# A decoder step with cached attention: each gate group's cache copy cut into eight pieces, and value sums placed in four column groups

## What is computed

```
def dilated_attention_step(q, k, v, cache, win, dil, rel_bias, h0):
    t = q.shape[1]
    lc = cache.shape[1]
    n_keys = win // dil + 1
    kv_all = jnp.concatenate([cache, jnp.stack([k, v], axis=2)], axis=1)
    idx = lc + jnp.arange(t)[:, None] - jnp.arange(n_keys)[None, :] * dil
    kvg = jnp.take(kv_all, jnp.maximum(idx, 0), axis=1)
    s = jnp.einsum('bthd,btjhd->bhtj', q, kvg[:, :, :, 0]) * SCALE + bias[:, None, :]
    p, lse = softmax_weights(s, None)
    o = jnp.einsum('bhtj,btjhd->bthd', p, kvg[:, :, :, 1])
    return o, jnp.moveaxis(lse, 1, 2), kv_all[:, t:]
...
pa = oa.reshape(b, s, A_OUT_W) @ w_oa
pb = ob @ w_ob
mix = (jax.nn.sigmoid(ga) * pa + jax.nn.sigmoid(gb) * pb) @ w_out
h = layer_norm(ALPHA * x + mix, ln1_g, ln1_b)
gate, up = jnp.split(h @ w_ffn_in, 2, axis=-1)
return layer_norm(ALPHA * h + (jax.nn.silu(gate) * up) @ w_ffn_out, ln2_g, ln2_b)
```

## Time and profile before

| | |
|---|---|
| median of 3 runs | 1805.73 us (1802.27 to 1807.96) |
| the profiled execution | 1798.35 us, its span 1796.6 us |
| TensorE busy | 1746.7 us, 97% of the span |
| VectorE busy | 993.2 us, 55% |
| ScalarE busy | 702.5 us, 39% |
| mean busy share of the 16 DMA engines | 44.2% for SyncE's queue (q1), 15.4% for ScalarE's (q10), 10.9% for GpSimd's (q0) |

### The profile page before, as it was taken

The page is one execution under the profiler, slowest core; times in us unless marked ns, Lnnn a source line. Parts: engine busy times, 40 slices in busy tenths (PEclk is TensorE's granted clock), DMA queues, the critical chain, the costliest instruction groups (busy, mean ns, idle before and its releaser), DMA issues.

```text
span 1796.6 us, 32525 instructions
## 1 busy us (share of the span) xinstructions
PE 1746.7 (97%) x12511; PEld 1661.9 (93%) x12511; DVE 993.2 (55%) x1397; ACT 702.5 (39%) x1041; POOL 124.3 (7%) x237
## 2 busy tenths in 40 slices
PE   8999999898999998999999999999999999999997
PEld 7999999765998987999989999999999999999996
DVE  4467677554386766575684444444444444444545
ACT  4343443354432333343453343334333333333333
POOL 1012222324010100000000000000000000000000
PEclk9999999998999999999999999999999999999999
DMA  6589999668788897668849888867765555556541
GB/s 215 153 274 316 326 318 340 179 172 271 238 278 314 284 317 252 197 220 256 262 149 304 254 254 250 265 210 237 251 220 164 164 164 162 167 165 210 161 159 53
DMA packets 204717, 410.75 MB, mean 229 GB/s; under 512 B 12220, under 2 KB 105686, under 8 KB 200416
## 3 DMA queue, kind: packets, MB, share of 16 engines
q1 hardware_dynamic: 178384, 254.41, 44.2%
q10 hardware_dynamic: 7488, 91.33, 15.4%
q0 software_dynamic: 18768, 63.94, 10.9%
HBM read 403.47 MB, written 94.92 MB: 277 GB/s over the span
## 4 chain that ended last, share of the span: by engine, by line
PE 90%; DVE 4%; DMA 3%; issue 1%; ACT 1%; SPq 0%; DVEq 0%; ACTq 0%; POOL 0%
PE bank L1284 87%; PE bank L1287 3%; DMA raw<-in_w_in_dram 2%; DVE wlo L888 1%; ACT whi L599 0%; DMA xs_s<-in_x_sample_dram 0%; DVE U L1198 0%; DMA KA<-in_cache_a_dram 0%; DVE PV L1081 0%; DVE U L1191 0%; DVE PV L1084 0%; ACT FT L624 0%; DVE SP L982 0%; DMA BIAS<-bias_scratch 0%; DVE RS L1217 0%
## 5 line engine op out<-in xcount | busy, mean ns | idle before, releaser
L888 DVE TENSOR_TENSOR wlo<-raw,whi 128x1024 fp32r<-128x1024 f32 x473 | 575.7, 1224 | 649.6 <-ACT whi L599 649.1
L599 ACT ACTIVATE whi<-raw 128x1024 fp32r<-128x1024 f32 x473 | 499.7, 1061 | 843.1 <-PE bank L1284 593.1
L1284 PE MATMUL bank<-X1H,whi 128*128 128x288 f32 x1408 | 417.0, 296 | 1.8 <-DVE X1L L1205 1.6
L1284 PE MATMUL bank<-X1L,whi 128*128 128x288 f32 x1408 | 415.4, 295 | 0.0
L1284 PE MATMUL bank<-X1H,wlo 128*128 128x288 f32 x1408 | 414.0, 294 | 0.0
L1284 PE MATMUL bank<-XH,whi 128*128 128x288 f32 x1248 | 375.0, 300 | 0.7 <-issue 0.6
L1284 PE MATMUL bank<-XL,whi 128*128 128x288 f32 x1248 | 369.4, 296 | 0.0
L1284 PE MATMUL bank<-XH,wlo 128*128 128x288 f32 x1248 | 368.1, 295 | 0.0
L1284 PEld LDWEIGHTS bank<-X1H,whi 128*128 128x128 f32 x1408 | 263.8, 187 | 2.5 <-issue 2.0
L1284 PEld LDWEIGHTS bank<-X1H,wlo 128*128 128x128 f32 x1408 | 265.1, 188 | 0.0
L1284 PEld LDWEIGHTS bank<-X1L,whi 128*128 128x128 f32 x1408 | 264.3, 188 | 0.0
(11 more groups left out here) (234 smaller groups left out, 1683.8 us busy)
## 6 DMA issues: line engine op xcount, KB each, us to landing
raw<-in_w_ffn_in_dram SPq DMA_DIRECT2D x176, 512.0 KB, 3.7
raw<-in_w_in_dram SPq DMA_DIRECT2D x156, 512.0 KB, 6.2
out_dram<-in_cache_b_dram ACTq DMA_DIRECT2D x28, 2336.0 KB, 11.7
raw<-in_w_ffn_out_dram SPq DMA_DIRECT2D x88, 512.0 KB, 4.1
KST<-in_cache_b_dram POOLq DMA_DIRECT2D x32, 512.0 KB, 4.8
QST<-tok_scratch POOLq DMA_DIRECT2D x32, 512.0 KB, 6.2
VST<-in_cache_b_dram POOLq DMA_DIRECT2D x16, 1024.0 KB, 11.8
raw<-in_w_out_dram SPq DMA_DIRECT2D x32, 512.0 KB, 5.0
```

The lines of the kernel that those rows point to most:

```text
L599: nc.scalar.activation(whi[s][:, :], raw[s][:, :], ACT.Copy).then_inc(hi_done, 1)
L888: nc.vector.tensor_tensor(wlo[s][:, :], raw[s][:, :], whi[s][:, :].bitcast(F32), ALU.subtract).then_inc(lo_done, 1)
L1284: return nc.tensor.matmul(out, lhsT, rhs, start=start, stop=stop, **kw)
```

## The change

Two parts. First, the copy that stood ahead of each gate group is issued as eight pieces, one ahead of every split. A piece is an eighth of the copy: `pieces=2`, shape 2 x 8 x 4672, 16 runs of 18,688 bytes; the total is the same. Second, the value sums: token t's matmul writes rows 32t to 32t + 31 of bank 6, with its weights in that group of 32 of the array's columns, and the four groups are added at the end by a new constant `FOLD` in place of a part of the identity. With it the order of value products changes: `PV` is started in step 1 and takes up `VST[0]` in step 2, which frees `VST[0]` two steps ahead of `VST[1]`, so that GpSimd may load its next values from there.

```diff
-        OROW = at("OROW", [NS, 512], 204288)
+        FOLD = at("FOLD", [P, NS], 204032)
+        OROW = at("OROW", [P, 512], 204288)
...
-                for g in (1, 2):
-                    if b >= 1:
-                        pool.wait_ge(pv_ready, b)
-                    pool.dma_start(VST[:, g - 1], caches[g][0, b].rearrange("(n r) k h d -> n r k (h d)", r=DIL[g])[:, 0:4, 1, :]
-                                   ).then_inc(v_in[g - 1], 16)
                 if b >= 2:
+                    pool.wait_ge(pv_ready, b - 1)
                     pool.wait_ge(cv_used, b - 1)
...
+                for g in (1, 2):
+                    if b >= 1:
+                        pool.wait_ge(*((vp_done, 4 * b - 1) if g == 1 else (pv_ready, b)))
+                    pool.dma_start(VST[:, g - 1], caches[g][0, b].rearrange("(n r) k h d -> n r k (h d)", r=DIL[g])[:, 0:4, 1, :]
+                                   ).then_inc(v_in[g - 1], 16)
...
             def gates(i):
-                copy_b3(i)
                 first = known_below(i, 1)
                 for k in range(8):
+                    shift(nb3_s[0], cache_b3[0], i * (73 * 1024) + k * (73 * 128), 73 * 128, 2)
                     split(PH_GATE, i, k)
...
+                nc.vector.tensor_reduce(FOLD[:, :], ident[:, :].rearrange("p (t n) -> p n t", t=DS), AX, ALU.add)\
+                    .then_inc(onecol_done, 1)
...
-                if step < 2:
-                    dve.wait_ge(v_in[step], 16 * b + 16)
-                    nc.vector.tensor_tensor(heads(VST[:, step]), heads(VST[:, step]), p(1 + step), ALU.mult).then_inc(vp_done, 1)
+                if step in (0, 3):
+                    g = step // 3
+                    dve.wait_ge(v_in[g], 16 * b + 16)
+                    nc.vector.tensor_tensor(heads(VST[:, g]), heads(VST[:, g]), p(1 + g), ALU.mult).then_inc(vp_done, 1)
                 elif step == 2:
                     dve.wait_ge(vp_done, 4 * b + 2)
-                    nc.vector.tensor_tensor(VST[:, 0], VST[:, 0], VST[:, 1], ALU.add).then_inc(vp_done, 1)
-                elif step == 3:
+                    nc.vector.tensor_tensor(PV[:, :, :], PV[:, :, :], VST[:, 0], ALU.add).then_inc(vp_done, 1)
+                elif step == 1:
...
-            nc.vector.tensor_copy(OROW[:, :], bank[6][0:NS, :]).then_inc(orow_done, 1)
+            nc.vector.tensor_copy(OROW[:, :], bank[6][:, :]).then_inc(orow_done, 1)
...
-                    ins = mm(bank[6][0:NS, :], ONECOL[:, NS - 1 - row:2 * NS - 1 - row], PV[:, t, :],
-                             row == 0, row == NS - 1)
+                    ins = mm(bank[6][NS * t:NS * t + NS, :], ONECOL[:, NS - 1 - row:2 * NS - 1 - row], PV[:, t, :],
+                             b == 0, b == DB - 1)
...
-                         OROW[:, P * pr:P * pr + P], ident[0:NS, 0:NS].unsqueeze(1).broadcast_to([NS, 2, NS]),
+                         OROW[:, P * pr:P * pr + P], FOLD[:, :].unsqueeze(1).broadcast_to([P, 2, NS]),
```

More of the change, by code:

```diff
@@ L559, in _ @@
                 pool.dma_start(CA[:, b % 2, :], cache_a[0, b, :, 1].rearrange("p h d -> p (h d)")).then_inc(cv_in[b % 2], 16)
-            pool.wait_ge(copy_out, 16 * (1 + 2 + 32 + 28))
+                for g in (1, 2):
[3 more added lines that the diff above has]
+                                   ).then_inc(v_in[g - 1], 16)
+            pool.wait_ge(copy_out, 16 * (1 + 2 + 32 + 20 + 64))
             pool.wait_ge(kv_out, 16 * 8)
@@ L1083, in value_products @@
                     dve.wait_ge(vp_done, 4 * b + 4)
-                    nc.vector.tensor_tensor(PV[:, :, :], PV[:, :, :], VST[:, 0], ALU.add).then_inc(pv_ready, 1)
+                    nc.vector.tensor_tensor(PV[:, :, :], PV[:, :, :], VST[:, 1], ALU.add).then_inc(pv_ready, 1)
             for k in range(8):
@@ L1525, in new_values @@
                 pe.wait_ge(vn_in, 32)
-                pe.wait_ge(onecol_done, 2)
+                pe.wait_ge(onecol_done, 3)
                 for pr in range(4):
```

## The result

The changed kernel takes **2029.76 us**, the median of 4 runs (2026.96 to 2033.44), beside 1804.9 for the kernel before on the same chip: a ratio of 1.1246, with a 95% interval of 1.1217 to 1.1276. That is 225 us slower. The profiled execution took 2027.24 us.

The account below looks back on a forecast made before the run. TensorE, 90% of the chain, was taken as the bound. Pieces at 8.05 us a chunk move the merge stage from 723.4 to 974, + 251 us: 1798.35 + 251 = 2049, 2057 as a median, stated as 2055; range 1950 to 2150.

Parts of the forecast that it names:

- Two engines, the same ones: Gate stage copy: each piece of two outer rows lies on the same two DMA engines; given 83%.
- the transfer in two waves of eight: GpSimd's 64 KB transfer to the output, 16 packets in two waves, read as outer dimension giving the number of shares.
- The pace of a chunk: Gate stage: a weight chunk takes 8.05 us on the crowded engines, with bounds of 7.3 and 9.8.
- The prediction's other sum, 8.4 us: Crowded engine's time for a chunk, added from copy runs 6.3, weight packets 1.4 and values 0.7 us.
- No copy put off: Gate stage: ScalarE can't run ahead, so one piece goes with one chunk and later stages stay as they are.
- The rival of copies that fall behind: Two engines, but weights pass at four to one and copies lie over later stages; 1870 to 1970 us, 5%.
- Swallowed: Gate stage: the value sums' gain, but for its tail, and the lower clock vanish since TensorE waits for chunks.
- Part 1 alone is 27.8 us: Value sums in column groups with the new product order: 17.9 us inside the gate stage, 9.9 at its end.
- The rival "no change": ScalarE's extra issues or the new steps eat up the value sums' gain of 28 us; below 1%.
- The wait of 5.06 us for PV falls: Gate stage's end: the new product order removes TensorE's wait, part of a 9.9 us gain that leaves 5.8 us.
- The signs: Profile marks expected in the gate stage, such as groups 60 to 70 us apart and a DMA share of about 0.4.

Follow-up runs that it names:

- e5: The changed kernel with pieces of 4 outer rows in place of 2; 1860.8 us, ratio 1.0317 to the kernel before.
- e7: The changed kernel with the pieces of 2 outer rows issued by GpSimd, all eight of a group ahead of its value loads; 1783.5 us.
- e2: The kernel before with only the copy cut into pieces of 2 outer rows; 2031.0 us, ratio 1.1281.
- e1: The changed kernel with each group's copy issued whole again, 16 outer rows, ahead of the group; 1797.9 us.
- e3: The changed kernel with the same eight pieces, each cut into 16 outer rows in place of 2; 1775.7 us.
- e12: The same kernel as e3, unchanged, measured again on another chip; 1771.2 us.
- e8: The kernel before with only the value sums in four column groups, copy whole, old order of loads and products; 1798.6 us.
- e11: The changed kernel with each group's copy in two halves of 16 outer rows, at chunks 0 and 4; 1774.2 us.
- e10: The kernel before with column groups and pieces of 16 outer rows, loads and products in the old order; 1779.0 us.
- e9: The kernel before with its copy in eight pieces of 16 outer rows, its own value sums and order of products; 1794.1 us.
- e4: The changed kernel with the pieces' two outer dimensions exchanged, 8 x 2 x 4672 in place of 2 x 8 x 4672; 1789.6 us.

## Why the prediction was right, and where it was not

**Two engines, the same ones: right.** Two outer rows put a piece on two engines (12.4% of sixteen, with no gap, and two short packets for each piece). That they are the same each time is concluded, since no trace names an engine: from e5, where four rows gave the time worked out for four fixed engines, and from e7, where a queue that doesn't hold to them brings the loss to nothing. The row that carried this was the transfer in two waves of eight: it had the number of shares. The step from there to "the same two" was a choice that no row carried, and it decided the sign.

**The pace of a chunk: right in kind, 5% too slow.** I had 8.05 us from 201 KB at 25 GB/s. From 475 us to the last sums at 943.09 it is 61 pieces and 7.67 us each. The term that was mis-sized is the rate. I read 0.82 us for a run where all sixteen engines copied at once, and 0.78 for a pair of packets where both queues filled them; with two engines busy a run alone takes 0.70 us. Then 8 x 0.70 + 16 x 0.08 (12.4% of 32 engine-us over 51 packets) + 0.65 for values, which seven of eight groups have, is 7.5 us. How much a run takes doesn't hang on the number of busy engines alone: in e7 all sixteen are full from 637 to 643 (77.3% + 25.0%), and a run takes 77.3% of 96 engine-us / 102 = 0.73 us there. What makes the 0.82 was not tried. The prediction's other sum, 8.4 us, counts eight of the sixteen weight packets twice, since each pair of rows 11 already holds one. Over 61 pieces 0.38 us is 23 us: the merge stage began at 950.3 in place of 974, and the median was 2030 in place of 2055. The reason given in the prediction, that memory isn't what limits two engines, was an argument for a faster rate than the rows show, and I kept the rate of the full engines.

**No copy put off: right.** There is no second loss behind the stage: after 950.3 the kernel runs 1074.5 us, and before it ran 1073.2 after 723.4. The rival of copies that fall behind is out; the one-to-one alternation that spoke against it shows in the changed kernel too (29 to 30).

**Swallowed: right, and more than I had.** e2 and the changed kernel are one time. The lower clock (mean 0.76 in the stage) is hidden as well: TensorE's work was 268 us of 485.

**Part 1 alone is 27.8 us: wrong as it stands.** With the copy whole it is 4 us (e1), and neither of its halves was sized wrongly. The sums take 1.06 us in place of 3.62, the last wait falls with even traffic, and both together give the 26 to 31 us of e3 and e12. What the step left out is that TensorE's time was also cover. (The rival "no change" got below 1% since nothing in the rows has the size of 28 us; in e1 the burst took 24 of them.) In the kernel before, sums stand where the copy's burst and the value loads hold up the weights (a copy at 678.29, sums at 687.9), and for 3.55 us of each group TensorE needed no chunk. With 2.55 of them gone it reaches the end of its lead: e1 and e8 wait 12 to 13 us for wlo, most of the 17.9 us that the sums give back. At 29.69 - 2.55 = 27.14 us a group the DMA engines are busy for 91% of 480 to 690 in e11; with the whole copy they are at 84% in e1. The reason, as I see it, is that the weights can run only three chunks ahead to make up for a burst. That the length of the burst decides is shown by e11, in which only the burst is halved; a longer lead was not tried. I had taken the same row (12.19 us for a chunk behind a copy) for covered because TensorE didn't wait then; by this account it was covered by the lead, three chunks of (29.69 - 3.55) / 8 = 3.3 us, and by the sums.

**The wait of 5.06 us for PV falls: wrong for part 1 alone, right with even traffic.** In the changed kernel 2.63 us of it are left, and the stage's end is 10.3 us where I had 8. The new order isn't enough (5.07 us in e1), even pieces aren't enough at the faster pace (3.97 in e10), both together are (none in e3, and a stage's end of 5.8 us, as I had worked out). At the pace of before, even pieces alone do it (e9).

**The signs.** Groups 60 to 70 us apart: 48 to 77, with a mean of 61 for the full ones, uneven because TensorE waits in long stretches behind GT. I hadn't seen that wait: the chunk that the last split of a group waits for is needed only three chunks later, but the sigmoids behind it free TensorE's banks. It moves waits about and adds next to nothing to the sum, since the load of the two engines gives 7.5 of the 7.67 us of a chunk. ScalarE's wait of some 400 us: 362. TensorE idle for over 200: 211. Landing: 27.1. DMA share of 0.4: 0.42. Eight matmuls of the sums in about 1 us: 1.06, and 1.94 at the stage's end at the lower clock. No wait for VST: 2.2 us.

## What to carry to other kernels

Before you cut a transfer into pieces, look at the outer dimension of each piece: on ScalarE's queue it was the number of engines, and always the same ones, so 2 rows in place of 16 cost 254 us here. A DMA share that falls while the bytes stay is the sign of it; multiply it by 16 in a starved stretch, and you have the engines at work. And when TensorE's work beside a burst gets shorter, ask what that work covered: two good changes (even traffic, short sums) gave 8 and 4 us alone (e9, e8), 23 together (e10), and 26 to 31 with the new order of products (e3, e12).

## What the runs showed that I had not expected

- One engine carries a run of 18,688 B in 0.70 us beside 14 idle ones, in 0.73 us with all sixteen full in e7, and in 0.82 us in another such stretch; why these two differ stays open.
- Dimensions that are neighbours in memory are joined: 8 x 2 x 4672 became 8 runs of 37,376 B (e4).
- A piece of two outer rows on GpSimd's queue goes round the engines (77.3% of sixteen busy in e7); on ScalarE's it does not (12.4%).
- Two halves of a copy are as good as eight pieces (1774.2 against 1771.2 and 1775.7 us).
